# A two-block network on one Trainium2 core: the front of the time mix and its triangular solves, reordered

## The chip, the core and the metric

The kernel runs on one NeuronCore of a Trainium2 chip. The core has a matrix engine (TensorE, PE in the profile; PEld is its weight load), a vector engine (DVE), an activation engine (ACT), GpSimd (POOL) and a queue engine (SP) that issues most transfers. Each engine runs its own list of instructions in order; they meet at semaphores. The metric is device time in microseconds (us) of one execution, lower is better. Three executions of the kernel before took 1459.95, 1461.27 and 1462.35 us (median 1461.27).

## The reference, cut to what matters

The reference is a small network on 256 tokens of width 1024, all in float32: an RWKV-7 time mix, a block-sparse attention, a second block with a gated recurrence and latent attention, and a layer of retrieved experts. The change lies in the time mix alone:

```
xx = shift(h) - h
r, wdn, k, v, adn, gp = [(h + xx*mu[i]) @ w_in[i] ...]     # widths 1024, 64, 1024, 1024, 64, 1024
decay = exp(-exp(-softplus(-(w0 + tanh(wdn) @ w2)) - 0.5)) # = exp(-e^-0.5 * sigmoid(...))
a  = sigmoid(a0 + adn @ a2)
kk = normalised per head (k * k_k);  k = k*(1 + (a-1)*k_a);  b = kk*a
for t in range(T):                                          # per head, S is 64 x 64
    sa = S @ kk[t]
    S  = S*decay[t] - outer(sa, b[t]) + outer(v[t], k[t])
    y[t] = S @ r[t]
y = groupnorm(y)*gn_w + gn_b + sum(r*k*r_k per head)*v
return (y * silu(gp)) @ w_out
```

## The kernel before, in words

The kernel does not step through the 256 tokens. It cuts them into two chunks of 128 (`c` or `t` = 0, 1) and solves each chunk in closed form. Sixteen heads of 64 features fill the width of 1024; a pair of heads fills 128 partitions when a tensor lies by feature.

All of `time_mix` is written once per engine (`pe`, `act`, `dve`, `pool`, `sp`), and each list's order is that of the Python code. PE results go to eight banks of PSUM, taken in turn by `claim`; `full(key)` marks a bank written, `filled` waits for that, `free(key)` says that a reader is done and `copied` waits for that. A `claim` waits until the bank's last user was freed. Weights come through a ring of eight slots of 512 KB that SP fills in the order of use (`load_weights`), waiting for each slot to be given back.

The stages of the time mix, in PE's order:

1. Keys: `project_keys`, 128x512 matmuls, 32 of them (the profile counts each float32 matmul as two records, so L435 x64).
2. The two low-rank projections `w` and `a` (L472): 16 matmuls with 64 stationary columns and 256 moving ones, all eight of `w` and then all eight of `a`. ACT takes them out with a tanh and a copy, and eight more matmuls (L484) make the arguments of the sigmoids `SIG` and `A`.
3. Values and receptance (`project`, L455), 64 matmuls.
4. Cumulative decay. `cum_in` and `cum_ex` (L495) multiply `SIG` by constant triangles, inclusive and exclusive, 4 matmuls each; ACT makes exponentials of both (`E`, `Ei` and `Ep`). `carry` (L500) is 16 matmuls with one moving column; it gives the factor, by feature, that carries the state from chunk 0 to chunk 1.
5. The gate projection `g` (L455 again), 32 matmuls.
6. The turns (L513): 64 transposes of 128x128 bring the four scaled factors (`a`, `r`, `k`, `b`) to lie by feature. DVE copies the even banks (L956), ACT the odd ones (L768). DVE's scaling (L940, L943) comes before.
7. `lower(0)` (L526, L536): the products inside chunk 0, masked by DVE (L1001 to L1013), `invert(0)` (L558 with L547 and L550 between): five levels of doubling that invert a unit triangle of 64x64 in each half of each head. Then `lower(1)`, `solve(0)`, `invert(1)`, `solve(1)`.
8. `solve(c)`: right sides `rhs` (L609), the inverse on the upper 64 rows (L622), what these give to the rows below (L637, added by DVE at L1038), the inverse on the lower 64 rows (L644), and the outputs: `values` (L628) and L652, 128x128 stationary blocks against 64 moving columns. In chunk 0 the state follows (L658, L659), with 64 stationary columns.
9. The group norm (`centre`, `vary`, `finish_y` on DVE with ACT), `turn_y` (L676), and the output projection (L684).

After that come the other three stages, which the change leaves as they are. The last one gathers expert rows by indirect DMA on POOL for some 650 us.

## Time and profile before

| | us |
|---|---|
| median of three runs | 1461.27 |
| profiled execution, device time | 1462.55 |
| its span, first to last instruction | 1460.7 |
| PE busy | 1317.9 (90%) |
| DVE busy | 842.9 (58%) |
| ACT busy | 421.4 (29%) |
| POOL busy | 294.1 (20%) |
| time mix, on the profile's clock | 0 to about 310 |

Times of rows are counted from the first instruction of that one execution. "Idle before" in a row is how long the engine stood still ahead of it, with the line that released it. A row of the chain of waits says what the end of the program hung on at that moment. PEclk is the granted TensorE clock, 1.00 for 2.4 GHz and 0.50 for 1.2 GHz.

### The profile page before, as it was taken

The numbers are of one execution on the slowest core, as the hardware profiler recorded it, in microseconds if no ns is written. First come the engines' busy times: TensorE is split into PE (matmuls) and PEld (weight loads), VectorE is DVE, ScalarE is ACT, GpSimd is POOL, SyncE is SP. The second block draws the span as 40 slices with busy tenths as digits, with TensorE's granted clock in tenths as the row PEclk, the third lists the DMA queues.
The fourth block names the chain that finished last, engine by engine and source line by source line (L and its number), as shares of the span: only waits on it lengthen the run. The fifth ranks groups of instructions, "written<-read, shape, count | busy, mean of one in ns | idle before, by whom it ended". The sixth has DMA issues, their size and how long they took to land.

```text
span 1460.7 us, 19081 instructions
## 1 busy us (share of the span) xinstructions
PE 1317.9 (90%) x7228; PEld 861.0 (59%) x7228; DVE 842.9 (58%) x2083; ACT 421.4 (29%) x971; POOL 294.1 (20%) x269
## 2 busy tenths in 40 slices
PE   7999999999999999999999988999877777878776
PEld 4445899988578887887789654454323333333322
DVE  7406667445654255433114776777877877777654
ACT  1203312122153116355002334333322322222222
POOL 0000000000000010000001334556544344444430
PEclk9999999999999999999999999999999999999999
DMA  8443100053322614522346999999999999999995
GB/s 318 134 157 127 34 3 4 1 173 130 123 97 73 208 60 165 168 90 87 132 161 234 422 421 420 419 421 421 421 422 421 421 421 422 420 421 421 422 421 241
DMA packets 66903, 368.02 MB, mean 252 GB/s; under 512 B 7229, under 2 KB 10685, under 8 KB 33725
## 3 DMA queue, kind: packets, MB, share of 16 engines
q0 software_dynamic: 37152, 269.50, 44.5%
q1 hardware_dynamic: 29518, 97.04, 19.6%
q8 instruction: 59, 0.97, 0.3%
q14 instruction: 30, 0.25, 0.1%
q10 hardware_dynamic: 144, 0.26, 0.0%
HBM read 365.73 MB, written 1.05 MB: 251 GB/s over the span
## 4 chain that ended last, share of the span: by engine, by line
PE 65%; DMA 24%; DVE 7%; ACT 2%; issue 1%; SPq 0%; DVEq 0%; ACTq 0%
PE bank L1657 16%; DMA cst<-peer_in,arena 12%; PE bank L2303 11%; DMA row<-peer_in,arena 7%; PE bank L455 6%; DMA arena<-peer_in,arena 5%; PE bank L2249 3%; PE bank L1195 3%; PE bank L558 3%; PE bank L1275 2%; PE bank L435 2%; PE bank L1252 2%; PE bank L684 2%; PE bank L1327 1%; PE bank L2237 1%
## 5 line engine op out<-in xcount | busy, mean ns | idle before, releaser
L2303 PE MATMUL bank<-arena 128*128 128x512 f32 x584 | 273.6, 609 | 61.0 <-ACT arena L2407 61.0
L2303 PEld LDWEIGHTS bank<-arena 128*128 128x128 f32 x584 | 109.0, 193 | 212.9 <-issue 212.6
L1657 PE MATMUL bank<-arena,ring 128*128 128x256 f32 (+2 forms) x1104 | 232.3, 371 | 2.2 <-DVE arena L2078 1.4
L1657 PEld LDWEIGHTS bank<-arena,ring 128*128 128x128 f32 x1104 | 198.8, 190 | 32.0 <-DVE arena L2078 1.8
L2544 DVE CUSTOM_DVE_ANT_0 arena<-arena 128x1024 f32<-128x1024 f32 x146 | 176.9, 1222 | 54.3 <-DMA arena<-peer_in,arena 54.2
L2589 POOL DMA_INDIRECT arena<-peer_in,arena x146 | 166.9, 1143 | 177.4 <-PE bank L2303 155.9
L2407 ACT ACTIVATE arena<-cst,arena 128x128 f32<-128x128 f32 x256 | 88.9, 394 | 133.4 <-DVE arena L2493 131.2
L2399 ACT ACTIVATE arena<-arena 128x2 f32<-128x2 f32 x129 | 38.1, 295 | 260.9 <-DVE arena L2544 260.7
L2303 PE MATMUL bank<-ring,arena 128*128 128x512 f32 x160 | 79.7, 644 | 22.1 <-ACT arena L2407 22.0
L455 PE MATMUL bank<-ring,arena 128*128 128x512 f32 x192 | 85.4, 607 | 0.0
L2589 POOL DMA_INDIRECT row<-peer_in,arena x18 | 19.9, 1106 | 313.8 <-DVE arena L2481 276.3
L2091 POOL COPY arena<-arena 64x2176 f32<-64x2176 f32 x2 | 4.0, 1995 | 388.6 <-DVE arena L1949 388.6
L2303 PE MATMUL bank<-cst,arena 128*128 128x512 f32 x140 | 68.0, 619 | 12.8 <-ACT arena L2407 12.7
L2303 PEld LDWEIGHTS bank<-ring,arena 128*128 128x128 f32 x160 | 31.3, 204 | 66.6 <-issue 66.6
L455 PEld LDWEIGHTS bank<-ring,arena 128*128 128x128 f32 x192 | 37.4, 195 | 47.1 <-issue 47.1
L2544 DVE CUSTOM_DVE_ANT_0 ring<-ring,arena 128x1024 f32<-128x1024 f32 x40 | 48.8, 1224 | 27.1 <-DMA ring<-peer_in,arena 27.1
L558 PE MATMUL bank<-arena 64*64 64x64 f32 x1792 | 55.5, 219 | 4.4 <-DVE arena L1029 2.3
L558 PEld LDWEIGHTS bank<-arena 64*64 64x64 f32 x1792 | 53.5, 135 | 7.9 <-DVE arena L1029 3.0
L2303 PEld LDWEIGHTS bank<-cst,arena 128*128 128x128 f32 x140 | 26.3, 194 | 50.2 <-issue 49.9
L2589 POOL DMA_INDIRECT ring<-peer_in,arena x40 | 40.7, 1018 | 58.0 <-PE bank L2303 53.7
L2544 DVE CUSTOM_DVE_ANT_0 cst<-cst,arena 128x1024 f32<-128x1024 f32 x35 | 42.7, 1223 | 13.0 <-DMA cst<-peer_in,arena 13.0
L2589 POOL DMA_INDIRECT cst<-peer_in,arena x35 | 40.9, 1167 | 43.1 <-PE bank L2303 41.0
(389 smaller groups left out, 1960.6 us busy)
## 6 DMA issues: line engine op xcount, KB each, us to landing
ring<-stream_in SPq DMA_DIRECT2D x155, 512.0 KB, 3.3
ring<-stream_in SPq DMA_DIRECT2D x8, 384.0 KB, 5.4
arena<-stream_in SPq DMA_DIRECT2D x6, 512.0 KB, 7.3
arena<-peer_in,arena POOLq DMA_INDIRECT x146, 33.3
row<-rows_in SPq DMA_DIRECT2D x4, 512.0 KB, 18.3
cst<-cst_in SPq DMA_DIRECT2D x1, 1933.0 KB, 17.1
row<-rows_in POOLq DMA_DIRECT2D x2, 512.0 KB, 4.9
cst<-rg_w_in SPq DMA_DIRECT2D x1, 1024.0 KB, 7.5
```

Source lines behind the costliest of these rows:

```text
L435: mm = nc.tensor.matmul(bank[:, :], mix["k"][:, k, t * P:(t + 1) * P], slot[:, i * 512:(i + 1) * 512], start=k == 0, stop=k == KT - 1)
L455: mm = nc.tensor.matmul(banks[t][:, :], mix[name][:, k, t * P:(t + 1) * P], slot[:, i * 512:(i + 1) * 512], start=k == 0, stop=k == KT - 1)
L558: mm = nc.tensor.matmul(bank[span(b), cols(j)], lhs(2 * j + p, b), rhs(2 * j + p, b), start=True, stop=True)
L684: mm = nc.tensor.matmul(bank, slot[:, k * P:(k + 1) * P], kT[:, k, t * P:(t + 1) * P], start=k == 0, stop=k == KT - 1)
L1195: mm = nc.tensor.matmul(bank[:, (m % 2) * T:(m % 2 + 1) * T], slot[:, k * P:(k + 1) * P], src[:, k, :], start=k == 0, stop=k == KT - 1)
L1657: mm = nc.tensor.matmul(bank[:, first:first + width], slot[:, at + k * cols:at + (k + 1) * cols], src[:, k, :], start=k == 0, stop=k == kt ...
L2249: mm = nc.tensor.matmul(bank[:, 0:T], slot[:, k * P:(k + 1) * P], n2[:, k, :], start=k == 0, stop=k == KT - 1)
L2303: mm = nc.tensor.matmul(core.banks[2 * t + b][:, :], diag[i % ND], value_half(i, b), start=False, stop=last)
L2399: nc.scalar.activation(act_out[:, part], dots[:, part], ACT.Gelu_apprx_tanh, scale=rstd[:, t:t + 1])\
L2407: nc.scalar.activation(diag[i % ND], cst("ident"), ACT.Copy, scale=act_out[:, i:i + 1])\
L2544: ins = nc.vector.tensor_tensor_reduce(out=row, in0=row, in1=half(X2, t), scale=1.0, scalar=0.0, op0=ALU.mult, op1=ALU.add, accum_out=dots ...
L2589: pool.indirect_dma_start(out=places[seat[i]], out_offset=None, in_=g.names["peer"], in_offset=bass.IndirectOffsetOnAxis(ap=index[:, i:i + ...
```

## The change

Eight edits in `time_mix`:

- The low-rank matmuls of `w` and `a` alternate, and `a` writes to partitions 64 to 127 of its bank, so the two use the left and the right half of the array. DVE makes their inputs in the same alternation.
- `cum_ex` and its constant are gone. DVE takes the own decay back off the inclusive sum (L1051 of the changed kernel), and ACT makes the exponential of that.
- The carry matmuls are gone. SP writes the last row of `E` of chunk 0 and the first row of `Ep` of chunk 1 to DRAM and reads them back by feature (16 elements in each of 128 partitions, each on its own); DVE divides one by the other after the turns and ahead of `lower(0)`, and waits for that transfer there.
- DVE's work on `R` (the bonus) goes in two halves behind the norm of the keys.
- The gate projection starts behind the four `cum_in` matmuls. Its first half and the first quarter of its second half run before the turns, one quarter between the turns of the two chunks, one behind them, one behind `lower(0)`. The second half keeps two banks all that time, which `pass_gate` steps over, so six are left for the rest. `weigh_gate(1)` moves on DVE behind `lower(0)`.
- In `solve`, the upper rows of half 1 alternate with the rows below of half 0, and the rows below of half 1 with the lower rows of half 0.
- The outputs `y` come by feature: `V` or `U` (64 columns) is stationary and the masked products (128 columns) move, with even heads on the left and odd heads on the right half of the array. They are turned back by 8 transposes a chunk (`turn_back`), in level 1 of `invert(1)` for chunk 0 and behind `turn_y(0)` for chunk 1, and ACT copies them once more (`keep_rows`).
- The state of chunk 0 goes in two parts, one between the groups of the solve and one at its end.

```diff
-        for n, name in enumerate(("w", "a")):
-            bank = claim(pe, ("lora", name))
-            for k in range(KT):
-                pe.wait_ge(mixed.handle, (n + 2) * KT + k + 1)
+        low = [claim(pe, ("lora", name))[n * LORA:(n + 1) * LORA, 0:T] for n, name in enumerate(("w", "a"))]
+        for k in range(KT):
+            for n, name in enumerate(("w", "a")):
+                pe.wait_ge(mixed.handle, 2 * KT + 2 * k + n + 1)
...
-        for kind in ("cum_in", "cum_ex"):
...
-        bank = claim(pe, "carry")
-        for j in range(KT):
-            for t in range(TT):
-                mm = nc.tensor.matmul(bank[:, j:j + 1], tok(SIG, t)[:, j * P:(j + 1) * P], cst("carry", t, t + 1),
-                                      start=t == 0, stop=t == 1)
-        mm.then_inc(*full("carry"))
-        project(3, "g")
...
+        def pass_gate():
+            while core.next_bank in [core.bank_at["g", t, 1][0] for t in range(TT)]:
+                core.next_bank = (core.next_bank + 1) % 8
...
+        gate_rows(0, range(4))
+        gate_rows(1, range(1))
+        turn_rows(0)
+        gate_rows(1, range(1, 2))
+        turn_rows(1)
+        gate_rows(1, range(2, 3))
...
             def values(half):
                 for i, h in enumerate(heads[half]):
-                    nc.tensor.matmul(y[half][:, cols(i)], LB[:, h, 2 * P:3 * P], tok(V, c)[:, cols(h)], start=i == 0, stop=False)
+                    nc.tensor.matmul(place_y(half, i), tok(V, c)[:, cols(h)], LB[:, h, 2 * P:3 * P], start=i < 2, stop=False)
...
+            for i in range(8):
+                mm = upper_rows(1, i)
+                if i == 7:
+                    mm.then_inc(*u_up.up())
+                mm = rows_below(0, i)
+            mm.then_inc(*full(("below", c, 0)))
...
         lower(0)
+        gate_rows(1, range(3, 4))
+        pass_gate()
         invert(0)
...
+            if t == 0:
+                turn_back(1)
             for quad in range(2):
                 copied(pe, ("turn", "y", t, quad))
...
+        dve.wait_ge(carry_loaded.handle, 16)
+        lk(nc.vector.reciprocal(small[:, KT:2 * KT], small[:, KT:2 * KT]))
+        lk(nc.vector.tensor_tensor(carry, carry, small[:, KT:2 * KT], ALU.mult))
...
         lower(0)
+        weigh_gate(1)
...
+        core.load_weights(sp, g.stream, core.slot_no[("g", 1, 3)] + 1)
+        sp.wait_ge(before.handle, 2 * TT)
+        sp.dma_start(g.carry_rows[0:1, :], tok(E, 0)[P - 1:P, :]).then_inc(*carry_kept.dma())
+        sp.dma_start(g.carry_rows[1:2, :], tok(Ep, 1)[0:1, :]).then_inc(*carry_kept.dma())
+        sp.wait_ge(carry_kept.handle, 32)
+        sp.dma_start(small[:, 0:2 * KT], g.carry_rows.rearrange("n (j p) -> p (n j)", p=P), allow_slow_non_contiguous=True)\
+          .then_inc(*carry_loaded.dma())
```

PE's list at the front, from the small constants to the first level of the inverse, in the kernel before. Here `x8` counts matmuls, not records; L455 is `g`, L513 the turns, L526 and L536 `lower(0)`.

```order
L495 MATMUL bank<-arena,cst 128x512 x8
L500 MATMUL bank<-cst,arena 128x1 x16
L455 MATMUL bank<-ring,arena 128x512 x32
L513 MATMUL bank<-cst,arena 128x128 x64
L526 MATMUL bank<-arena 128x128 x16
L536 MATMUL bank<-arena 64x64 x32
L558 MATMUL bank<-arena 64x64 x32
```

The same place in the changed kernel: L509 is the gate, L532 the turns, L557 and L571 `lower(0)`, L593 the first level.

```order
L495 MATMUL bank<-arena,cst 128x512 x4
L509 MATMUL bank<-ring,arena 128x512 x20
L532 MATMUL bank<-cst,arena 128x128 x32
L509 MATMUL bank<-ring,arena 128x512 x4
L532 MATMUL bank<-cst,arena 128x128 x32
L509 MATMUL bank<-ring,arena 128x512 x4
L557 MATMUL bank<-arena 128x128 x16
L571 MATMUL bank<-arena 64x64 x32
L509 MATMUL bank<-ring,arena 128x512 x4
L593 MATMUL bank<-arena 64x64 x32
```

Four of eight triangle matmuls and the 16 of the carry are gone, the gate's 32 are spread from the triangles to behind `lower(0)`, and nothing else is new there.

PE's list in `solve(0)` of the kernel before, from the right sides to the state (L658 and L659 go on in turn):

```order
L609 MATMUL bank<-arena 128x64 x16
L622 MATMUL bank<-arena 64x64 x16
L628 MATMUL bank<-arena 128x64 x8
L637 MATMUL bank<-arena 64x64 x16
L628 MATMUL bank<-arena 128x64 x8
L644 MATMUL bank<-arena 64x64 x16
L652 MATMUL bank<-arena 128x64 x16
L658 MATMUL bank<-arena 64x64
L659 MATMUL bank<-arena 64x64
```

The same in the changed kernel, up to the first pairs (L666 upper rows, L679 `values`, L670 rows below; the pair goes on eight times):

```order
L651 MATMUL bank<-arena 128x64 x16
L666 MATMUL bank<-arena 64x64 x8
L679 MATMUL bank<-arena 64x128 x8
L666 MATMUL bank<-arena 64x64
L670 MATMUL bank<-arena 64x64
L666 MATMUL bank<-arena 64x64
L670 MATMUL bank<-arena 64x64
```

The counts of products are the same; what changed is the shape of `values` (64 output partitions by 128 columns) and which neighbours stand side by side.

DVE's list between the copies of the turns and the first level in the changed kernel (L1075 the copies, L1077 and L1078 the carry, L1122 to L1134 `lower(0)`, L1068 `weigh_gate(1)`, L1141 the masks of level 1):

```order
L1075 COPY arena<-bank 128x4x128 x8
L1077 RECIPROCAL small<-small 128x8
L1078 TENSOR_TENSOR small<-small 128x8
L1122 TENSOR_TENSOR arena<-bank,cst 128x4x128 x2
L1128 COPY_PREDICATED arena<-cst,bank 128x8x64
L1122 TENSOR_TENSOR arena<-bank,cst 128x4x128 x2
L1128 COPY_PREDICATED arena<-cst,bank 128x8x64
L1133 COPY_PREDICATED arena<-cst,arena 64x8x64
L1134 COPY_PREDICATED arena<-cst,arena 64x8x64
L1133 COPY_PREDICATED arena<-cst,arena 64x8x64
L1134 COPY_PREDICATED arena<-cst,arena 64x8x64
L1068 TENSOR_TENSOR arena<-bank,arena 128x512 x2
```

The two carry instructions stand where nothing stood, with the wait for the transfer ahead of them, and the two gate products came here from ahead of the copies.

## Rows read from the trace of the kernel before

**Rows 1.** The page's chain that ended last, shares of the span by engine.
```profile
PE 65%; DMA 24%; DVE 7%; ACT 2%; issue 1%; SPq 0%; DVEq 0%; ACTq 0%
```
**Rows 2.** A window of 100 us: busy time by engine, PEclk, DMA share, GB/s.
```profile
800.00:900.00 100.00, 91.53 (x315) 55.24 (x315) 72.14 (x206) 35.67 (x83) 41.73 (x37) 0.98 1.01 420
```
**Rows 3.** The chain of waits, 40 to 151 us: start, duration, engine and line.
```profile
40.34 7.05 PE bank L472 x32
...
54.45 54.93 PE bank L455 x128
109.39 6.87 PE bank L495 x16
116.25 4.23 PE bank L500 x32
120.48 30.17 PE bank L455 x64
```
**Rows 4.** Windows around the carry matmuls and over the turns.
```profile
116.00:118.00 2.00, 2.00 (x19) 1.91 (x18) 1.90 (x4) 2.00 (x5) 0.00 (x0) 1.00 0.00 0
...
120.00:122.00 2.00, 2.00 (x5) 1.16 (x5) 1.97 (x2) 1.46 (x2) 0.00 (x0) 0.50 0.00 0
...
150.00:158.00 8.00, 7.64 (x66) 7.05 (x64) 6.18 (x10) 5.11 (x9) 0.00 (x0) 1.00 0.21 66
```
**Rows 5.** PE's instructions in order of time: start, duration, line, shapes.
```profile
150.49 7.15 PE L513 MATMUL bank<-cst,arena 128*128 128x128 f32 x64
158.37 1.83 PE L526 MATMUL bank<-arena 64*128 64x128 f32 x28 [0.73 <-DVE arena L956]
```
**Rows 6.** PE's waits up to 310 us: total, times, longest.
```profile
PE bank L558 <- DVEq L1009: 2.0, 2, 1.0
```
**Rows 7.** ACT's instructions in order of time, behind the low-rank matmuls of `w`.
```profile
43.97 0.38 ACT L732 ACTIVATE arena<-bank 64x256 f32<-64x256 f32 x1 [1.70 <-PE bank L472]
```
**Rows 8.** Chain of waits, 195 to 280 us: both solves.
```profile
201.42 3.71 PE bank L609 x32
205.13 2.00 PE bank L622 x32
207.14 1.93 PE bank L628 x16
...
215.01 3.71 PE bank L652 x32
...
220.78 2.01 PE bank L558 x64
...
255.34 1.93 PE bank L609 x16
...
277.99 2.02 PE bank L684 x16
```
**Rows 9.** PE groups up to 310 us by shape: busy us, mean ns, idle before.
```profile
L526 PE MATMUL bank<-arena 64*128 64x128 f32 x64 | 4.1, 278 | 0.7 <-DVE arena L956 0.7
L658 PE MATMUL bank<-arena 128*64 128x64 f32 x32 | 2.0, 226 | 0.0
```
**Rows 10.** DVE in order of time, at the end of the second solve.
```profile
267.82 0.69 DVE L1038 TENSOR_TENSOR arena<-arena,bank 64x512 f32<-64x512 f32 x1 [0.24 <-PE bank L637]
...
271.35 1.23 DVE L990 TENSOR_TENSOR arena<-arena 128x1024 f32<-128x1024 f32 x1
```
**Rows 11.** DVE in order of time, at the front.
```profile
110.12 2.29 DVE L926 TENSOR_TENSOR arena<-arena 128x2048 f32<-128x2048 f32 x1 [43.78 <-ACT arena L724]
...
128.11 3.49 DVE L943 TENSOR_TENSOR arena<-arena 128x1024 f32<-128x1024 f32 x3
...
159.60 1.51 DVE L1001 TENSOR_TENSOR arena<-bank,cst 128x512 f32<-128x512 f32 x2 [1.67 <-PE bank L526]
```
**Rows 12.** DMA in the first 320 us: a queue's share, and an issue's time to landing.
```profile
q1 hardware_dynamic: 10281, 31.87, 29.1%
...
vec<-vec_in SPq DMA_DIRECT2D x1, 79.5 KB, 3.9
```

More of the change, by code:

```diff
@@ L521, in lower @@
             for m in range(2):
-                banks = [claim(pe, ("la", c, p, m)) for p in range(2)]
+                banks = []
+                for p in range(2):
+                    if not c:
+                        pass_gate()
+                    banks.append(claim(pe, ("la", c, p, m)))
                 for i in range(4):
@@ L591, in solve, with place_y @@
             at = slice(c * P, (c + 1) * P)
-            def by_state(bank, which, half, stop):
-                for i in range(4):
-                    j = 4 * half + i
-                    mm = nc.tensor.matmul(bank[:, i * P:(i + 1) * P], ar[:, j, which, at], state[:, j, :], start=False,
-                                          stop=stop and i == 3)
-                return mm
+            def place_y(half, i):
+                return y[half][span(i % 2), i // 2 * P:(i // 2 + 1) * P]
             heads = [range(8 * half, 8 * half + 8) for half in range(2)]
@@ L611, in solve @@
                 if c == 1:
-                    mm = by_state(rhs[half], 0, half, True)
+                    for i in range(4):
+                        j = 4 * half + i
+                        mm = nc.tensor.matmul(rhs[half][:, i * P:(i + 1) * P], ar[:, j, 0, at], state[:, j, :], start=False, stop=i == 3)
                 mm.then_inc(*full(("rhs", c, half)))
@@ L640, in solve @@
-            values(1)
-            for half in range(2):
-                copied(pe, ("below", c, half))
-                for i, h in enumerate(heads[half]):
-                    mm = nc.tensor.matmul(u[half][span(1), cols(i)], XT[c][span(1), h, :], RHS[span(1), cols(h)], start=True,
-                                          stop=True)
-                mm.then_inc(*full(("u", c, half)))
-            if c == 0:
-                bank = claim(pe, "state")
+                    nc.tensor.matmul(place_y(half, i), tok(V, c)[:, cols(h)], LB[:, h, 2 * P:3 * P], start=i < 2, stop=False)
@@ new lines, in from_state, with state_part @@
+            def from_state(half):
+                for i in range(4):
+                    j = 4 * half + i
+                    nc.tensor.matmul(y[half][:, i * P:(i + 1) * P], state[:, j, :], ar[:, j, 1, at], start=False, stop=False)
+            def state_part(lhs, rhs, first):
+                for h in range(H):
+                    j, q = place[h]
+                    mm = nc.tensor.matmul(state_bank[q:q + HD, j * HD:(j + 1) * HD], lhs[:, cols(h)], rhs[:, cols(h)],
+                                          start=first and j == 0, stop=not first and j == KT - 1)
+                return mm
@@ new lines, in solve @@
+            mm.then_inc(*full(("below", c, 0)))
+            values(1)
+            pe.wait_ge(u_top.handle, 2 * c + 2)
+            copied(pe, ("below", c, 0))
+            below[1] = claim(pe, ("below", c, 1))
+            for i in range(8):
+                mm = rows_below(1, i)
+                if i == 7:
+                    mm.then_inc(*full(("below", c, 1)))
+                mm = lower_rows(0, i)
+            mm.then_inc(*full(("u", c, 0)))
+            if c == 1:
+                from_state(1)
+            else:
+                state_bank = claim(pe, "state")
+                state_part(tok(K, 0), tok(V, 0), True)
@@ L649, in solve @@
+            copied(pe, ("below", c, 1))
+            for i in range(8):
+                mm = lower_rows(1, i)
+            mm.then_inc(*full(("u", c, 1)))
             for half in range(2):
@@ L943, in _, with weigh_gate @@
                 nc.vector.tensor_tensor(tok(dst, t), tok(dst, t), tok(by, t), ALU.mult).then_inc(*scaled.up())
-        for half in range(2):
+        def weigh_gate(half):
             for t in range(TT):
```

186 lines of the change are left out of this document (127 added, 59 removed).

## The prediction, written before the changed kernel ran

> **What bounds the kernel now.** I read the page's chain first: 65% of the span hangs on PE [rows 1]. The other large share is DMA, and it lies late, where the gathers fill the DMA engines (share 1.01 from 800 to 900 us) [rows 2]. So a microsecond that PE saves in the time mix should move the whole rest of the program forward, gathers included, since the first gather waits for indices that come down PE's chain. The chain in order of time shows what the time mix consists of [rows 3, 8]: PE follows PE with hardly anything between, so its own durations are the sum to work with. Then the waits: in the front PE stands still ahead of `lower(0)` (0.73 us) [rows 5] and twice, 2.0 us together, ahead of the first level of the inverse [rows 6].
>
> **The parts on the path.**
>
> Low-rank projections: 16 matmuls take 7.05 us [rows 3]. In the changed order `w` and `a` sit on the two column halves. The pattern that shows what this is worth is the state, 32 matmuls with 64 stationary columns and 64 moving ones, two of one half and then two of the other: L658 takes 2.0 us and L659 runs inside the same 2.1 us (218.65 to 220.78) [rows 8, 9], so 0.067 us each, where the 64x64 matmuls of L622, all on one tile, take 2.00 / 16 = 0.125 [rows 8]. Halves therefore run side by side, and 7.05 becomes 3.53. But `w` used to be ready 3.5 us before `a`, with its tanh hidden there. Now the tanh (0.38 us, started 0.1 after the matmul) [rows 7] is bare: with both handovers about 0.7 us of wait. The gain is 3.5 - 0.7 = 2.8.
>
> Triangles and carry: half of 6.87 us and all of 4.23 us go [rows 3]: 3.4 + 4.2 = 7.7 rounded. The own decay is taken off on DVE and the exponentials are as many as before. Behind these, PE now goes into the gate, so their lateness counts only against the first turn.
>
> Clock: the gate's 64 records take 30.17 us, against 54.93 / 2 = 27.47 for as many records of the same shape just before [rows 3]. The granted clock is 1.00 from 116 to 118 us, in the carry's matmuls with one moving column, and 0.50 (1.2 GHz) from 120 to 122 [rows 4]. With the carry gone I expect no fall there: 2.7.
>
> Gate rows moved: no work is added, but one quarter (4 matmuls at 27.47 / 32 = 0.86, 3.4 us) lies ahead of `lower(0)` and covers the 0.73 us wait, and another lies behind it and covers the 2.0 us ahead of level 1 [rows 5, 6]: 2.7. If that cover failed, these 2.7 are lost and no more. DVE gets the two products of `weigh_gate(1)` ahead of the masks of level 1, 0.69 each at the price of its nearest row [rows 10], 1.4 in all. The quarter behind `lower(0)` brings PE 3.4 us of work and hides 2.0, so PE comes 1.4 us later to level 1's second half as well, and I cost this at nothing; uncovered it is 1.4.
>
> Are the turns late? PE reaches them 20 gate matmuls (17.2 us) behind the triangles. In before's times shifted by the 2.8, receptance ends at 106.6, the triangles at 110.0 and the turns may begin at 127.2. DVE's bonus used to start at 110.12 and its scaling ended at 131.6 [rows 11]. An operation over 2048 columns costs 2.29 and one over 1024 costs 3.49 / 3 = 1.16 [rows 11]. Now the norm (two of 2048) and half the bonus are done before the last of `R` arrives at about 107.3. Behind it come the other half (three of 1024, 3.6 with their handovers), four subtractions of 512 columns (0.8 each), and four of 1024 a chunk (4.8), so the first turn's inputs stand at about 119, both chunks' at 124. Slack 8 us. During the turns six banks go round in place of eight; PE fills one in 7.15 / 16 = 0.45, ACT and DVE empty them in turn at the same pace, and the block ran without a wait [rows 5]; nothing.
>
> `solve(0)`: 201.42 to 220.78, 19.4 us [rows 8]. New terms: right sides 3.71, unchanged. Upper rows of half 0 and lower rows of half 1 alone, 8 matmuls at 0.125 each: 2.0. Two blocks of 16 alternating 64x64 matmuls: at the state's rate of two tiles side by side, 1.0 each, 2.0. Outputs: four blocks of 8 with 128 moving columns. L628 takes 1.93 per block of 8 and L652 3.71 for two [rows 8]. The changed shape isn't in the trace; the nearest is L526, 128 moving columns and two row halves side by side, 4.1 us for 32 matmuls [rows 9], 0.128 each. The bounds are half of L628's price (0.12, perfect pairs) and all of it (0.24, no pairs). I take 0.128: 4 x 1.03 = 4.1. State 2.1 unchanged in sum. Total 13.9, gain 5.5.
>
> `turn_back(0)`: 8 transposes at 7.15 / 64 = 0.112 [rows 5], 0.9 us in level 1 with the path through PE. Cost 0.9.
>
> `solve(1)` to the output projection: 255.34 to 277.99, 22.7 us [rows 8]. The same edits give 5.5 again. But `turn_y(0)` needs `finish_y(0)`, which stands on DVE behind the second addition from below. From that addition's start to the end of L990 it takes 271.35 + 1.23 - 267.82 = 4.8 us [rows 10]; before, it was ready at 272.6, well ahead of the projection. Now only 4.0 us of PE work (the products with the state, one group of lower rows, the outputs) follow the addition's release, so a new wait of about 1.0 us ends on DVE. `turn_back(1)` takes 0.9 us beside the copies of `turn_y(0)`, which PE waits for anyway; I allow 0.2. Gain 5.5 - 1.0 - 0.2 = 4.3.
>
> Handovers inside the solves: each addition by DVE (0.69) [rows 10], and each copy by ACT at about the same, has a block of 1.0 us of PE work to hide in, with 0.2 to 0.3 of semaphore time. That is just level; for each of the six I allow 0.1, together 0.6.
>
> Sum: 2.8 + 7.7 + 2.7 + 2.7 + 5.5 - 0.9 + 4.3 - 0.6 = 24.2 us. Against the profiled execution (1462.55, 1.3 above the median) that is 1438.4; against the median of 1461.27 it is 1437.1. I predict 1437.
>
> **The carry's transfer, costed at nothing.** SP waits for the last exponential (about 115 us in the shifted times), writes two rows, waits, and reads 16 x 128 elements one by one. DVE waits for it behind the turns' copies, at about 138.7 (127.2, the turns' 7.15, a gate quarter and the last copy), and everything of `lower(0)` on DVE is queued behind that wait; PE and ACT wait for that in turn. DVE had 1.67 us idle at that place [rows 11], and the gate quarters behind give PE 3.4 more. So the chain has some 25 us in all; with two landings of 3.9 us each [rows 12] the element-wise read may take about 20 before anything is late. No row shows such a read. From below it is an ordinary landing, 3.9. From above, 10281 packets took 29.1% of 16 engines' 320 us [rows 12], 0.145 us each at a mean of 3.1 KB; 2048 packets at that price over 16 engines are 18.6 us. Both ends fit. The Trainium skill (DMA: Bandwidth & Descriptors, Rules for kernel authors) says that a non-contiguous last dimension is lowered to one descriptor for each element and tells authors to avoid it; no run here shows its price yet, and it is why I keep this as a rival.
>
> **Rivals.**
>
> 1. Column halves with 128 moving columns do not run side by side. For it: each half streams all 128 partitions of its own moving operand, and that at 128 columns is not in the trace. Against: L658 and L659 do it at 64 columns [rows 9]. Price: low-rank 3.5, outputs 8 blocks x 8 x 0.11 = 7.2, the alternating upper/below blocks 2.0, less the 1.0 wait on `finish_y`: 11.7 less gain, 1449. A milder form stands in the Trainium skill (TensorE: Matmul & The Clock Gate, Part 3, What overlaps and what doesn't): a weight load is hidden by a running matmul only if the row group differs, and here both halves use all rows. The low-rank rows speak against it: 7.05 / 32 = 0.220 us a record [rows 3], and half of a record of 512 columns (54.93 / 128 / 2) is 0.215, which leaves no room for a bare load. As a mechanism of this kernel a bare load of 64 columns costs at most the 0.0625 us of a 64x64 record [rows 8]: 64 output matmuls x 2 records x 0.0625 / 2 and 32 low-rank records / 2 x 0.0625, 5.0 together, 1442.
>
> 2. The clock falls somewhere else, behind the turns or in the solves, where small matmuls are denser than before. Against: it stays at 1.00 over 7.15 us of transposes [rows 4]. Price the same 2.7: 1440.
>
> 3. The element-wise read is slow; this ends on the other side. It turns into a loss when it takes longer than 20 + 24 = 44 us, so from 0.34 us an element on 16 engines, or 0.021 on one. If all 2048 elements went through one engine at 0.145, it would take 297 us and the kernel 1461 - 24 + 277 = 1714. Against: the read's destination is 128 partitions, like that of all loads here that use the engines evenly.
>
> 4. The front's gain is given back later: weights come too late for a PE that is 24 us earlier. Against: SP's waits are for slots that PE itself frees, so they shift with it, and DMA is idle in the solves. Price perhaps half: 1449.
>
> **How the numbers follow.** Forecast as summed 72%, its own range 1433 to 1441; rival 1 in full 6%, in its mild form 6%; rival 2 7%; rival 3 4%; rival 4 3%; the rest something not seen. The range 1431 to 1447 holds the forecast, rival 2 and the mild rival 1. Two runs differ by about 0.2% (3 us) for no reason, so faster means below 1458.4. Only rival 3 or something not seen reaches that: faster 94%, same 2%, slower 4%.
>
> **What would show it.** In the changed trace: L472's block 3.5 us, followed by a wait on ACT of 0.5 to 1; no PEclk under 1.00 around 110 to 130; no PE wait ahead of `lower(0)` or level 1; output blocks (L679, L733) of 1.0 us per 8; about 1 us idle ahead of L764 on DVE; DVE not idle on `small<-carry_rows` ahead of L1077. The output projection starts at about 253.5 in place of 277.99. If L679's blocks take 1.9 the pairs are wrong; if DVE waits for the carry, part of the gain goes there; if the projection starts at 253 and the end does not move by 24, the sum was right and my reading of the later stages wrong.

## The result, and the profile after

| kernel | device time, us | runs |
|---|---|---|
| before | 1461.81 (1459.95 to 1464.89) | 4 |
| changed | 1438.3 (1437.14 to 1440.26) | 4 |
| before, timed again | 1462.91 (1462.16 to 1463.54) | 9 |
| changed, timed again | 1438.53 (1438.01 to 1439.91) | 5 |

The ratio is 0.9836, with a 95% interval of 0.9823 to 0.9849. In the second timing, taken later, it is 0.9833 (0.9820 to 0.9846). The forecast was 1437, inside a range of 1431 to 1447; the medians lie 23.5 us apart, where 24.2 were forecast. The kernel before, timed beside other experiments, also gave 1464.39 us (7 runs) and 1468.01 (one run), so only kernels timed together are compared. The profiled execution took 1439.42 us, with a span of 1437.3 against 1460.7 before. Times below are read from these two traces unless another kernel is named.

The page's chain by engine, for [rows 1], has hardly moved, and the gather stage is as full as in [rows 2]:

```profile
PE 64%; DMA 24%; DVE 8%; ACT 2%; issue 1%; SPq 0%; DVEq 0%; ACTq 0%
```

```profile
800.00:900.00 100.00, 90.72 (x270) 48.91 (x269) 77.62 (x225) 34.98 (x83) 43.41 (x38) 1.00 1.01 421
```

The chain of waits from 38 to 60 us (start, duration, engine and line) answers to the first of [rows 3]. The low-rank matmuls keep their line, L472:

```profile
39.95 3.61 PE bank L472 x31
...
43.59 0.39 ACT arena L822
...
44.25 7.11 PE bank L485 x16
```

7.05 us became 3.6, and a tanh that used to be hidden now stands bare on ACT. From the first low-rank matmul to the values projection it was 54.45 - 40.34 = 14.1 us before and is 51.36 - 39.95 = 11.4 now, a gain of 2.7.

The same view from 100 to 150 us answers to the rest of [rows 3] and to [rows 5]. L495 makes the triangles, L509 the gate, L532 the turns, L557 and L571 `lower(0)`, L593 the inversion:

```profile
106.29 3.43 PE bank L495 x8
109.72 17.17 PE bank L509 x40
126.89 3.49 PE bank L532 x32
...
137.31 3.44 PE bank L509 x8
140.75 1.99 PE bank L557 x32
142.74 1.09 PE bank L571 x64
143.83 3.63 PE bank L509 x8
147.46 2.01 PE bank L593 x64
```

No wait stands in it. From the triangles to `lower(0)` it was 158.37 - 109.39 = 49.0 us and is 140.75 - 106.29 = 34.5. Between the turns' two parts stands one more gate quarter. The granted clock (the last column but two, between the busy times and the DMA share) answers to [rows 4]. In the kernel before it had begun to fall inside the carry's one-column matmuls (116.25 to 120.48) and stood at 0.50 behind them. Of before, the window that [rows 4] leaves out:

```profile
118.00:120.00 2.00, 2.00 (x15) 2.00 (x14) 2.00 (x1) 0.86 (x2) 0.00 (x0) 0.69 0.00 0
```

The changed kernel stays at 1.00 in every window of 2 us from 100 to 132; one of them:

```profile
118.00:120.00 2.00, 2.00 (x6) 0.90 (x5) 2.00 (x2) 0.00 (x0) 0.00 (x0) 1.00 0.88 92
```

The chain from 180 to 256 us answers to [rows 8]. The output blocks are L679 and L733, the state L689, the 64x64 blocks L666 to L675. Between 190.91 and 194.09 the left-out rows are the single matmuls of two alternating blocks:

```profile
185.09 3.72 PE bank L651 x32
188.81 1.07 PE bank L666 x16
189.88 1.02 PE bank L679 x16
...
191.98 1.02 PE bank L679 x16
...
194.09 1.08 PE bank L689 x32
...
196.24 1.90 PE bank L733 x32
...
199.07 2.01 PE bank L593 x64
...
234.64 1.93 PE bank L651 x16
...
246.59 0.69 DVE arena L1159
...
250.12 1.24 DVE arena L1111
251.41 1.09 PE bank L764 x8
252.50 0.87 PE bank L745 x8
253.37 2.66 PE bank L774 x23
```

`solve(0)` took 19.36 us and takes 199.07 - 185.09 = 13.98. From `solve(1)` to the output projection 22.65 became 253.37 - 234.64 = 18.73. At the end of it DVE is on the path, with the last scaling of the outputs (L1111) behind the addition from below (L1159), which answers to [rows 10]. PE's waits from 30 to 270 us (total, times, longest) answer to [rows 6]:

```profile
PE bank L593 <- DVE arena L1150: 2.3, 2, 1.1
PE bank L764 <- DVE arena L1111: 0.8, 1, 0.8
...
PE bank L485 <- ACT arena L822: 0.7, 1, 0.7
```

The 2.0 us on DVE's queue are gone. The 2.3 were there before, under L1029.

The carry, for [rows 11, 12]: the issue with its time to landing, and DVE's first operation that needs it, with no wait noted in brackets behind it.

```profile
small<-carry_rows SPq DMA_DIRECT2D x1, 8.0 KB, 3.1
```

```profile
137.52 0.19 DVE L1077 RECIPROCAL small<-small 128x8 f32<-128x8 f32 x1
```

### The profile page after: what moved, and what is told of

Same layout as the page of the kernel before. It is cut to its first block, busy times and chain, and to the rows that moved or that the text cites. A ratio compares the mean times of both kernels' runs of the same rounds, so it can differ in the third digit from the quotient of the medians.

```text
span 1437.3 us, 19059 instructions
## 1 busy us (share of the span) xinstructions
PE 1292.8 (90%) x7204; PEld 840.5 (58%) x7204; DVE 847.1 (59%) x2093; ACT 423.6 (29%) x974; POOL 294.2 (20%) x269
## 4 chain that ended last, share of the span: by engine, by line
PE 64%; DMA 24%; DVE 8%; ACT 2%; issue 1%; SPq 0%; DVEq 0%; ACTq 0%
PE bank L1785 16%; PE bank L2431 11%; DMA cst<-peer_in,arena 10%; DMA arena<-peer_in,arena 10%; DMA row<-peer_in,arena 5%; PE bank L455 4%; PE bank L2377 3%; PE bank L1323 3%; PE bank L593 3%; PE bank L1403 2%; PE bank L435 2%; PE bank L509 2%; PE bank L1380 2%; PE bank L774 2%; DVE arena L2672 1%
## 5 line engine op out<-in xcount | busy, mean ns | idle before, releaser
L2431 PE MATMUL bank<-ring,arena 128*128 128x512 f32 x160 | 77.2, 623 | 22.9 <-ACT arena L2535 22.9
L2431 PEld LDWEIGHTS bank<-ring,arena 128*128 128x128 f32 x160 | 29.8, 195 | 66.0 <-issue 66.0
L593 PE MATMUL bank<-arena 64*64 64x64 f32 x1792 | 55.3, 219 | 2.4 <-DVE arena L1150 2.3
L593 PEld LDWEIGHTS bank<-arena 64*64 64x64 f32 x1792 | 53.4, 135 | 6.3 <-DVE arena L1150 3.0
L455 PE MATMUL bank<-ring,arena 128*128 128x512 f32 x128 | 55.1, 592 | 0.0
L1323 PE MATMUL bank<-arena,ring 128*128 128x256 f32 x224 | 49.5, 379 | 0.0
```

The source lines that it names most:

```text
L455: mm = nc.tensor.matmul(banks[t][:, :], mix[name][:, k, t * P:(t + 1) * P], slot[:, i * 512:(i + 1) * 512], start=k == 0, stop=k == KT - 1)
L593: mm = nc.tensor.matmul(bank[span(b), cols(j)], lhs(2 * j + p, b), rhs(2 * j + p, b), start=True, stop=True)
L1323: mm = nc.tensor.matmul(bank[:, (m % 2) * T:(m % 2 + 1) * T], slot[:, k * P:(k + 1) * P], src[:, k, :], start=k == 0, stop=k == KT - 1)
L2431: mm = nc.tensor.matmul(core.banks[2 * t + b][:, :], diag[i % ND], value_half(i, b), start=False, stop=last)
```

## The experiments

Most experiments change a few microseconds, near what two runs differ by, and nine of the twelve ran only once (1438.76 to 1445.90 us). Each is therefore read by one stretch of its own trace, from the first low-rank matmul to the first of the output projection. What lies behind the stretch varies by more than many of the effects: from the first gather to the end of the span it is 665.5 to 671.6 us in the fourteen traces. By PE's instructions in order of time the stretch up to the output projection is 237.7 us before, 213.34 in the changed kernel and 213.30 in its repeat. Every profiled stretch includes the same work unless the text says otherwise. Instructions in order of time are shown as in [rows 5]. A matmul leaves two records in the counts, a transpose one.

**Do column halves run side by side? Low-rank products, one half after the other.**

```diff
-        for k in range(KT):
-            for n, name in enumerate(("w", "a")):
+        for n, name in enumerate(("w", "a")):
+            for k in range(KT):
```

> The changed kernel with the low-rank matmuls of w all ahead of those of a, still on the two column halves. I read the stretch from the first low-rank matmul to the start of the output projection (213.4 us in the changed kernel, 237.7 before). Theory: two column halves run side by side only when their matmuls alternate, so the block takes 7.05 us in place of 3.6, the wait for the tanh (0.7) goes, and the stretch is 2.8 longer, 216.2. Rival (the 64-column shape on separate halves is itself cheaper, whatever the order): block 3.6 to 4, stretch 213 to 214.

```profile
41.04 6.31 PE L472 MATMUL bank<-arena,ring 128*64 128x256 f32 x32
```

The stretch was 215.25 us, 1.9 longer, and the run 1443.29. The block rose to 6.25 us from its start to the next, not to the 7.05 of before, and the wait on ACT went. So the order is what pairs the halves, but one change of half in the middle already buys 7.05 - 6.25 = 0.8 us. At 0.220 us a record that is between three and four records of each half that ran together.

**The same in groups of four**, to see whether that overlap comes at each change of half.

```diff
-        for k in range(KT):
-            for n, name in enumerate(("w", "a")):
+        for n, name, k in [(n, name, k) for ks in (range(0, 4), range(4, 8)) for n, name in enumerate(("w", "a")) for k in ks]:
```

> The changed kernel with the low-rank products in groups of four: four matmuls of the one half of the columns, four of the other, and again. In the changed kernel they alternate one by one (32 records in 3.6 us); in the kernel with the one half after the other it is 6.25 us, which is 29 records one after another at 0.215, so three records overlapped at the single change of half. If that is a rule (matmuls start in order, and about three may stand ahead of the one that runs), three changes of half overlap 9 records: 23 x 0.215 = 4.95 us. By the rival (nothing but immediate neighbours overlaps, one matmul of two records at each change) it is 26 x 0.215 = 5.6 us; by a second (both halves run freely side by side) 3.6 us as in the changed kernel.

```profile
39.88 4.70 PE L472 MATMUL bank<-arena,ring 128*64 128x256 f32 x32
44.51 7.13 PE L485 MATMUL bank<-arena 65*128 65x512 f32 x16
```

44.51 - 39.88 = 4.63 us. With three changes of half, (7.05 - 4.63) / 0.220 = 11 records overlapped, 3.7 at each; with one change it was 3.6. The overlap does come at every change, a little larger than the three I had put in. The rival with one matmul per change (5.6 us) falls, and so does free running (3.6). The block is 1.0 us longer than in the changed kernel, but the wait of 0.7 on ACT is gone, as `w` ends earlier, so the stretch is only 0.3 longer (213.64).

**Output matmuls, the even heads and then the odd ones.**

```diff
-                for i, h in enumerate(heads[half]):
+                for i in (0, 2, 4, 6, 1, 3, 5, 7):
+                    h = heads[half][i]
...
```

(and likewise for the products with `U`)

> The changed kernel with its output matmuls in another order: in each block of eight the four heads that go to one column half come first and then the four of the other half, where the changed kernel alternates the halves; the work is the same. Eight blocks of 128x64 with 128 moving columns are touched, 1.07 to 1.10 us each in the changed kernel's trace. If the alternation is what halves them (the theory of the forecast), each block rises towards the 2 x of one half after the other, by up to 0.9 us, less the overlap of the two halves where they meet, which the low-rank run showed to be some 0.7 us in 7; the block that stands before a wait of 0.8 us hides part. The stretch from the low-rank products to the output projection grows from 213.4 us by 3.5 to 6.5. If instead the output shape alone (64 columns out of 128 stationary rows) makes them cheap and the halves don't overlap (rival), the stretch stays within 0.5 us of 213.4.

```profile
190.39 1.58 PE L680 MATMUL bank<-arena 128*64 128x128 f32 x16
...
251.78 2.57 PE L735 MATMUL bank<-arena 128*64 128x128 f32 x32
```

In the changed kernel these entries read 1.09 and 1.97. So the blocks of eight matmuls rise by 0.49, four times, and the two double blocks by 0.6 each: 3.2 us, of which 0.6 hide in the wait ahead of the last turn, which shrank from 0.8 to 0.2. The stretch grew by 2.5 to 215.86. The pairing of halves with 128 moving columns is real, and rival 1 is out. Both halves write one bank here, where `w` and `a` write two, so it is not the change of bank that pairs them. My expectation of 3.5 to 6.5 was too high because it put 0.9 on a block; the overlap at each change of half takes nearly half of that back, as in the two runs above.

**Upper or lower rows of one half and rows below of the other, one set after the other.**

```diff
-                if i == 7:
-                    mm.then_inc(*u_up.up())
-                mm = rows_below(0, i)
+            mm.then_inc(*u_up.up())
+            for i in range(8):
+                mm = rows_below(0, i)
```

(and likewise for the rows below of half 1 with the lower rows of half 0)

> The changed kernel with the two sets of eight of the solve's value rows one after the other, where the changed kernel alternates a matmul for the upper rows or the lower rows of one half of the heads with one for the rows below of the other half. Four such double blocks stand in the two solves, at about 1.1 us for 16 matmuls. By the theory (two matmuls on different column halves run side by side) each comes to about 2 us, so the stretch of 213.4 us grows by 3 to 3.8; the copy of the first set can then start half a block earlier, which takes back up to 0.5 us at each. By the rival (the two sets need different operands, and the time is set by loading these, side by side or not) the stretch stays within 0.5 us.

```profile
191.10 0.97 PE L666 MATMUL bank<-arena 64*64 64x64 f32 x13
191.86 0.27 PE L670 MATMUL bank<-arena 64*64 64x64 f32 x1
...
192.08 0.92 PE L670 MATMUL bank<-arena 64*64 64x64 f32 x13
192.93 1.09 PE L679 MATMUL bank<-arena 128*64 128x128 f32 x16
```

The double block takes 192.93 - 191.10 = 1.83 us in place of 1.07. The rows show the overlap itself: thirteen records of one set, then three of each in turn, then thirteen of the other. Four such blocks cost 3.0 us; the wait of 0.78 ahead of the last turn took back its part. The stretch grew by 2.2 (215.55), below my 3 to 3.8, since I had that wait stay. My expectation called all four blocks pairs of column halves. By the code only L666 with L670 is one; L670 with L675 reads different halves of the rows (partitions 0 to 63 and 64 to 127) and writes the same half of the columns. Both kinds gain alike: 1.08 us in alternation, and 1.83 and 1.82 one set after the other (195.78 - 193.96 in `solve(0)`). So the theory holds, and for row halves too.

**What made the clock fall? Sixteen matmuls with one moving column put back ahead of the gate,** and **the same with 128.** Before had as many carry matmuls at this place with one column. The wide kernel has `[:, 0:128]` and `cst("cum_in", 0, 128)` in the two places; the weights are the same in both, and no later work uses the results.

```diff
+        extra = claim(pe, "extra", 7)
+        for j in range(KT):
+            for t in range(TT):
+                mm = nc.tensor.matmul(extra[:, 0:1], tok(SIG, t)[:, j * P:(j + 1) * P], cst("cum_in", 0, 1),
+                                      start=True, stop=True)
...
```

> The changed kernel with 16 matmuls added behind the triangles, as the old carry had them: 16 weight loads of 128 columns, one moving column each; their result is not used. Theory of the clock: the granted clock falls to 0.5 some microseconds into them or behind them, the 20 gate matmuls that follow lose about 2.7 us, and the stretch grows by 4.3 + 2.7 = 7.0 to 220.4. Rival (the fall before had another cause, such as the run of triangles and copies together): 4.0 to 4.3 and no fall, 217.6. Total 1438.3 + 7 = 1445 by the first, 1442.5 by the second.

> As the run with 16 added matmuls of one moving column, but each moves 128 columns; the weight loads are the same. Theory: what lets the clock fall is an array that hardly moves columns, so here it stays at 1.00, the block takes 16 x 0.227 = 3.7 us and the stretch is 217.1. Rival (the weight loads, back to back, are what does it): a fall to 0.5 as with one column, and 219.8.

The narrow kernel's matmuls, then its windows:

```profile
109.52 3.63 PE L501 MATMUL bank<-cst,arena 128*128 128x1 f32 x32
113.01 19.11 PE L516 MATMUL bank<-ring,arena 128*128 128x512 f32 x40
```

```profile
114.00:116.00 2.00, 2.00 (x3) 0.67 (x2) 1.85 (x3) 1.80 (x2) 0.36 (x1) 0.50 0.01 4
116.00:118.00 2.00, 2.00 (x5) 0.90 (x4) 2.00 (x3) 0.12 (x1) 1.90 (x4) 0.77 0.16 1
```

The wide kernel's:

```profile
110.20 3.73 PE L501 MATMUL bank<-cst,arena 128*128 128x128 f32 x32
113.77 17.33 PE L516 MATMUL bank<-ring,arena 128*128 128x512 f32 x40
```

```profile
114.00:116.00 2.00, 2.00 (x6) 0.84 (x5) 1.71 (x2) 1.71 (x3) 0.00 (x0) 1.00 0.00 0
```

Both added blocks keep PE occupied for 3.5 us. Behind the one with one moving column the clock falls to 0.50 (1.2 GHz) and the gate's 40 records take 1.8 us more (19.11 against 17.33); behind the one with 128 columns it stays at 1.00 (2.4 GHz). The weight loads are the same in both, so these alone do not bring the fall. Each kernel was traced once, and one run further down shows a fall at another place that its edit does not explain. What speaks against chance here is that both traces with one-column matmuls (this one and before) show a fall at this place, and none of the twelve others does.

The size was not met. The stretch grew by 5.2 (218.57) where the theory said 7.0 and the rival 4.0 to 4.3; the wide one's grew by 3.6 (216.92), as expected. The added block took 3.5 us in place of before's 4.2, in which the clock was already falling, and the fall cost 1.8 in place of 2.7. So 1.7 us of the 6.9 that the carry cost before did not come back with it, and why is open. Timed, the narrow kernel took 1447.16 us (1442.99 to 1449.46, 4 runs), a ratio of 0.9881 (0.9853 to 0.9910) to the 1464.39 of the kernel before beside it, wider spread than any other.

**Both gate quarters ahead of `lower(0)`.**

```diff
-        lower(0)
         gate_rows(1, range(3, 4))
+        lower(0)
```

> The changed kernel with the last gate quarter ahead of the first lower() in place of behind it. Theory: PE then waits twice for DVE ahead of level 1, as before, 2.0 to 2.3 us together, and the stretch is 215.6. Rival (DVE, freed of the gate's products a little earlier, catches up, or the waits come back only in part): under 214.4.

```profile
PE bank L593 <- DVE arena L1150: 2.6, 3, 1.1
PE bank L593 <- DVEq L1130: 2.0, 2, 1.0
```

The 2.0 us of [rows 6] are back. The stretch grew by 2.9 (216.25) where 2.2 were expected: 0.3 more is a third wait on L1150. The other 0.6 is in no wait of this view, but it lies where the waits are: from `lower(0)` to the end of level 1 PE takes 2.3 us more and in level 2's block 0.8 more, where the waits noted are 2.0 and 0.3, and the gate takes 0.2 less. The quarter behind `lower(0)` is what covers the waits ahead of level 1.

**How much slack has the carry? The read eight times in a row.**

```diff
-        sp.dma_start(small[:, 0:2 * KT], g.carry_rows.rearrange("n (j p) -> p (n j)", p=P), allow_slow_non_contiguous=True)\
-          .then_inc(*carry_loaded.dma())
+        for n in range(8):
+            sp.dma_start(small[:, 0:2 * KT], g.carry_rows.rearrange("n (j p) -> p (n j)", p=P), allow_slow_non_contiguous=True)\
+              .then_inc(*carry_loaded.dma())
+            sp.wait_ge(carry_loaded.handle, 16 * (n + 1))
...
-        dve.wait_ge(carry_loaded.handle, 16)
+        dve.wait_ge(carry_loaded.handle, 16 * 8)
```

> The changed kernel with the element-wise read of the two carry rows made eight times in a row, each waiting for the one before, and VectorE waiting for the last. One read lands 3.1 us after its issue at 116.4 us, so eight come to about 116.4 + 8 x 3.1 to 3.5 = 141 to 144 us. By the theory the single read has some 17 us of slack (VectorE comes to its wait at 137.5): eight reads make a wait of 4 to 7 us there, of which the matmuls beside it hide 3 to 4, and the stretch of 213.3 us grows by 0 to 4. By the rival (element-wise reads are slow when the queues are full of other work) a read costs 6 us or more and the stretch grows by over 20 us.

The eight issues in order of time, then DVE's wait:

```profile
116.46 25.01 SPq L1274 DMA_DIRECT2D small<-carry_rows  x8
```

```profile
DVE small L1077 <- DMA small<-carry_rows: 6.2, 1, 6.2
```

The 25.01 us reach from the first issue to the last, at 141.1. DVE's wait ended at 143.9, so eight reads took 27.4 us, 3.4 each with the issue. From issue to landing the single reads took 2.7 us at least, 3.0 in the median and 5.0 at most: the first took 3.1 us; the second, issued at 119.6 while weights came in (DMA share 0.99 from 120 to 122), 5.0; the fourth, issued at 127.5, 4.7, though no more than 6 GB/s moved from 124 to 132; the rest 2.7 to 3.0. What made the fourth slow is not known. Even 5.0 is below the 6 us of the expectation's rival. DVE waited 6.2 us, and of these 1.5 reached the stretch (214.83). Rival 3 needed 44 us for one read and is out by a distance.

**The wait that the change made: the first half's last scaling moved ahead of the addition from below on DVE.**

```diff
+            if c == 1:
+                finish_y(0)
             add_below(c)
...
-            if c == 1:
-                finish_y(0)
         def lay(t):
```

> The changed kernel with VectorE's last scaling of the first half's outputs moved ahead of the addition of the rows below in the second half. In the changed kernel TensorE waits 0.8 us for it at the first turn of the outputs in the last solve; by the theory the three operations (1.24 us each) are then done before that point, while VectorE would otherwise be idle, and the stretch shortens from 213.4 by 0.7 to 1.0 us. By the rival the addition of the rows below is itself late by the 3.7 us of the three operations, and the wait only moves to the rows below or to the copies of U: no gain, or up to 3 us slower.

The wait at L764 is gone and the stretch is 0.9 shorter (212.46), as the theory had it. DVE does the three operations in time that it spent idle before.

**A wait that was there all along: DVE's preparation of gate and bonus rows, spread over the levels.**

```diff
-                if (c, lev) in ((0, 3), (1, 1)):
-                    prepare(1 - c)
+                share = {(0, 1): (0,), (0, 2): (1,), (0, 3): (2,), (0, 4): (3,), (1, 1): (0, 1), (1, 3): (2, 3)}
+                if (c, lev) in share:
+                    prepare(1 - c, share[c, lev])
...
```

> The changed kernel with VectorE's preparation of the gate and bonus rows (four operations in a row, after which TensorE waits 1.13 us twice in the block of the inversions) given out one or two at a time over the levels of the two inversions. By the theory both waits go and the stretch shortens from 213.4 by 2.0 to 2.3 us. By the rival each single operation makes a wait of its own, as VectorE's copies set each level's pace: four to six waits of 0.3 to 0.6 us, and the stretch stays within 0.5 us or grows.

The stretch came out 3.5 us longer (216.83), and by that number alone the theory would have fallen. The trace says otherwise. Here its windows by the low-rank second matrices and the values:

```profile
44.00:46.00 2.00, 1.34 (x3) 0.68 (x4) 1.98 (x5) 1.94 (x3) 0.00 (x0) 1.00 0.53 141
...
48.00:50.00 2.00, 2.00 (x4) 0.81 (x3) 2.00 (x7) 0.73 (x2) 0.00 (x0) 0.50 0.00 0
...
60.00:62.00 2.00, 2.00 (x5) 0.91 (x4) 1.97 (x2) 0.00 (x0) 0.00 (x0) 0.76 0.00 0
```

The clock fell here for some 14 us, far ahead of anything that the edit touches, and cost 6.8 us: from L485's start to the triangles 68.66 against 61.88. From the inversion's first matmul (L593) to the output projection this kernel takes 102.57 us, the changed one 105.84. Both waits on L1150 are gone and 3.3 us with them, more than the 2.3 noted as waits. The rest lies around the waits too. In the changed kernel the level that holds the first one runs from 172.68 to 181.95:

```profile
177.76 4.26 PE L593 MATMUL bank<-arena 64*64 64x64 f32 x128 [1.13 <-DVE arena L1150]
```

That is 9.27 us against 7.63 for the same level unbroken, 1.64 for a wait of 1.13; the 128 records behind the wait took 4.19 where half of the unbroken block is 3.82. Why they are slower the rows don't say. The kernel below has the same edit on DVE and no such fall of the clock, so the fall is not the edit's.

**Both edits together, timed beside the changed kernel itself.**

> The changed kernel with both of the edits on VectorE together: the last scaling of the first half's outputs ahead of the addition of the rows below, and the preparation of the gate and bonus rows given out over the levels of the inversions. By the theory these are two separate waits, so the gains add: 0.9 us of the one (measured alone) and 3.3 of the other (the blocks from the first inversion to the output projection took 105.8 us in the changed kernel and 102.6 with this edit alone), 4.2 together: the stretch of 213.3 us comes to about 209.2, and the time to 4 us under the changed kernel's on the same chip. By the rival the gather stage behind, which is bound by its transfers, gives most of it back: under 1.5 us in the median.

> The changed kernel itself once more, on the chip of the kernel beside it. By the theory 23 to 24 us under the kernel before (a ratio of 0.984), the stretch from the low-rank products to the output projection 213.3 us, and no fall of the clock ahead of the masks of the inversion, in contrast to the kernel before. By the rival (that the gain was partly the chip's or the moment's) the ratio moves out of 0.982 to 0.985.

```profile
172.92 7.70 PE L593 MATMUL bank<-arena 64*64 64x64 f32 x256
```

The level that had broken in two is one block of 7.70 us. The stretch is 209.19 us against 213.30 in the repeat: 4.1, as the sum of the two said. The time is 1435.37 us (1433.52 to 1436.59, 5 runs) against 1438.53, with ratios to before of 0.9814 (0.9801 to 0.9827) and 0.9833 (0.9820 to 0.9846). The medians lie 3.2 apart and the single runs don't overlap, though the two intervals do. It is the fastest kernel of this study, and neither of the two profiled executions shows a clock under 1.00 in the stretch.

## Why the prediction was right, step by step

- **Low-rank products, 2.8.** Measured 2.7: 3.4 from the pairs, less a wait of 0.7 on ACT. Halving the block was right for the reason given, as the runs in groups show.
- **Triangles, carry, clock and gate quarters, 7.7 + 2.7 + 2.7.** Together 13.1; measured 14.5 to `lower(0)`, less 1.3 by which the block behind it grew (from `lower(0)` to the inversion's second part 8.9 before, 10.2 now, with 3.6 of gate in it): 13.2. No wait was left at either place. The clock term is backed by the pair with 1 and 128 columns, though put back alone the narrow block gave only 1.8 of the 2.7. The 4.2 for the carry's matmuls held some of the clock as well: at 1.00 as many take 3.5. Why before's fall began earlier and lasted longer stays open.
- **The turns, 8 us of slack.** The first turn's inputs stood at 118.9 and both chunks' at 123.5, as worked out (119 and 124), and the turns began at 126.9. DVE was late for nothing.
- **`solve(0)` 5.5, `solve(1)` the same, handovers -0.6.** `solve(0)` gave 5.38, handovers included, so the 0.6 was not needed: the sum had 4.9 to 5.2 there. 0.128 us per output matmul, taken from the state's and L526's pairs, was measured at 1.02 / 8 = 0.128. The experiment on the order of the heads shows that it is pairing.
- **`turn_back(0)`, -0.9.** Measured 1.02.
- **`solve(1)` to the projection, 4.3.** Measured 3.9, and its parts are off both ways. PE's last block of the solve ended at 276.38 before, with the first turn behind it:

```profile
276.38 0.46 PE bank L676 x4
```

So the solve itself took 276.38 - 255.34 = 21.0 us before. Now it ends ahead of the wait for L764, at 251.41 - 0.78 = 250.63, and takes 250.63 - 234.64 = 16.0, a gain of 5.05 and not 5.5. The two blocks of products with the state that stand between the outputs rose from 0.95 to 1.09 us each (L596 before, L684 now), which I had as unchanged, and the 64x64 blocks take 1.07 or 1.08 where I had 1.0. The wait on `finish_y(0)` was 0.8, not 1.0. From the first turn to the projection it was 277.99 - 276.38 = 1.6 and is 253.37 - 251.41 = 2.0: `turn_back(1)` costs 0.35 net where I allowed 0.2. Its 0.87 stands in the chain at 252.50, but PE's wait of 0.73 for DVE's copy at this place is gone.
- **The carry at nothing.** Right, with room: the chain was over before 120 us (issue at 116.4, 3.1 us to land), and DVE came to it at 137.5. My bounds for the read were 3.9 and 18.6; the truth lay below the lower one. The Trainium skill (DMA: Bandwidth & Descriptors, Rules for kernel authors) says to rearrange such a read so that its last dimension is contiguous. For 2048 elements, with this much slack, DVE's wait for the read is nothing in the changed kernel, so there was nothing here for that to gain.
- **Rival 1 in its mild form.** By the Trainium skill (TensorE: Matmul & The Clock Gate, Part 3, What overlaps and what doesn't) loads on the same rows would not hide behind a running matmul. Here all tiles of an output block use all rows, and the block takes 0.128 us per matmul, the same as the two-row-half block of [rows 9]. The trace does not agree with a price for that.
- **Rival 2.** The clock stayed at 1.00 in the changed kernel's turns, inversions and solves. The fall in one later run (the spread preparation) came at another place and cost 6.8 us, where the rival has 2.7. It stands in one trace of fourteen; that the changed kernel's had none is luck as far as is known.
- **Rival 4.** By the chain of waits the stretch shrank by 237.65 - 213.42 = 24.2 us, which is the 24.2 forecast. The projection started 24.6 earlier, the first gather 25.2 (795.0 to 769.8), the span ended 23.4 earlier. The 1.8 lost in the gather stage is within the 6 us that this stage varies by; in the second timing the medians lie 24.4 apart. No part of the gain was given back that these runs can show.

So the mechanisms were right term by term, and no term is off by more than 0.6. That the sum met the measured one to a tenth is luck: the handovers of 0.6 did not come, and the front gave 0.1 more; against them `solve(1)` with its end gave 0.4 less, and `solve(0)`, `turn_back(0)` and the low-rank products 0.1 less each.

## What to carry to other kernels

Matmuls that use half of the columns, or half of the rows, are worth pairing by order alone. Strict alternation is best for the block, but each change of half already overlaps three to four records: groups of four gave 2.4 of the 3.4 us here, and the order of groups can be chosen for what the next engine needs first. When such a change shortens PE's work, look at what DVE does in a row just before each handover; here moving three operations and spreading eight brought 4 us. Judge a change of a few microseconds by a stretch of the trace with its clock beside it: one kernel here read 3.5 us slower over a stretch in which its own edit had saved 3.3.

## What the runs showed of the hardware that I had not expected

- Halves overlap by about 3.6 records at each change of half, whether there is one change (6.25 us for 32 records) or three (4.63), against 7.05 unpaired and 3.6 in strict alternation. With 64x64 tiles, column halves and row halves pair alike (1.08 us for 32 records, against 1.83 and 1.82 one set after the other).
- PE fully occupied by one-column matmuls for 3.5 us is followed by a granted clock of 0.50; the same count with 128 columns is not (one trace each). The Trainium skill (TensorE: Matmul & The Clock Gate, Part 4: PE-mode transpose) says that the fast clock does not engage for transposes, since they do not count as busy in the same way. The trace does not agree: before's 64 transposes ran for 7.15 us with the clock at 1.00 [rows 4, 5], and the changed kernel's two blocks of 3.5 us as well.
- A clock fall can also come without the edit's doing: in one run a wait of 0.66 us at 44 us was followed by 14 us near 0.50, and a wait of 0.66 to 0.69 at the same place by none in the changed kernel, its repeat and the fastest kernel. What decides it was not found.
- The read of 2048 elements of 4 bytes, one by one, lands in 2.8 to 3.3 us when it is made once (twelve traces), and in 2.7 to 5.0 us when it is made eight times in a row.
- A wait of 1.13 us on PE cost 1.6 in the block's length; the records behind it are slower, for a reason that was not found.
